# Moving VectorE's mixing weights and two engines' loop numbers behind the first block of a mixture-of-experts loop

## The chip, the cores and the metric

The kernel runs on one core of a Trainium2 chip. The metric is the device time of one execution in microseconds; where several runs are given, their median is meant.

## The reference

A decoder trunk of two layers over 512 tokens of width 1024, in float32. The first layer mixes tokens by a convolution, the second by dilated attention. Behind each mixer stands a mixture of experts: 16 experts in 4 groups, each token takes one group and the best two experts in it.

```python
def hierarchical_moe(h, r_grp, r_exp, w_gate, w_up, w_down):
    p_grp = jax.nn.softmax(t @ r_grp);  g_idx = argmax(p_grp);  p_top = p_grp[g_idx]
    sel = expert logits of the group g_idx
    top_v, top_i = lax.top_k(sel, 2)
    w_in = jax.nn.softmax(top_v, axis=-1) * p_top[:, None]     # the mixing weights
    a = t @ w_gate[e];  u = t @ w_up[e]
    y = sum over e of (silu(a) * u * gates[:, e]) @ w_down[e]
```

The mixing weights are two numbers a token, `w_in`. They are needed only when the experts' outputs are added up.

## The kernel before

The experts are computed in blocks of 128 token slots; each block has one expert. There are at least 16 blocks, and more where an expert has over 128 tokens; how many is known only when the routing has been computed on the chip. So the routing (`routing`, on VectorE) leaves three integers in SBUF, `two_i` and `last_i` (two columns), and each engine reads them into its own registers with `value_load`: `two`, `last` and `before`. `before` is the number of trips of the main loop, `last` the number of the last pair of blocks, `two` says whether the last pair is whole. SyncE, GpSimd and TensorE have their own loads; the change leaves these alone.

Every product is made in three passes: an operand is cut into a leading part (fp32r, made by ScalarE: `gate_lead`, `up_lead`, `rows_lead`, `down_lead`) and a trailing part (VectorE: `gate_trail`, `up_trail`, `rows_trail`, `down_trail`), and TensorE adds lead x lead, lead x trail and trail x lead. Blocks go in order 0, 1, 2, ...; block 0 has its gate and up products ahead of the loop (TensorE's `gate(0, 0)`, `up(0, 0)`). After that a `split_block(i, c)` takes, on each engine, the gate and up products of block 2i + c and the down product of the block before it. TensorE's order in it is: gate, transposed rows of the next block, first half of the down product, up, second half of the down product, transposition of the hidden values. Half a down product needs from ScalarE `hTh` and `wdh`, and from VectorE `hTl` (waited for at its start) and `wdl` (waited for ahead of its last four matmuls, L2081).

The engines run from instruction lists of their own and are tied only by semaphores. All instructions of an engine run in the order of its list, so a pause on VectorE delays all that stands behind it there. `wgh` is one buffer: ScalarE may refill it only when the gate product that reads it is done. VectorE's small steps in `mixing_weights` (L1561 to L1568) wait for each other through the semaphore of `steps`, so that its sequencer can't run ahead of them.

The loop's body (both `split_block(i, 1)` and `split_block(i, 2)`) is in a `Fori` loop of the engine. On VectorE and TensorE the loop began at pair 0; on ScalarE pair 0 was written out and the loop began at 1.

Of the kernel before, what the change touches and what calls it, by code (L numbers as in the profile page):

```python
# [47 lines left out]
E = 16  # L48
# [5 lines left out]
XB = 8  # L54
# [89 lines left out]
def build_program(nc, a):  # L144
# [7 lines left out]
    with ExitStack() as ctx:  # L152
# [3 lines left out]
        def sem(name):  # L156
            return ctx.enter_context(nc.semaphore(name))
# [148 lines left out]
        def rs(*dims, dt=F32):  # L306
            nonlocal o
            n = 1
            for d in dims:
                n *= d  # L310
            ap = cut(HTQf, o, *dims)
            o += n
            return ap.bitcast(dt) if dt != F32 else ap
# [47 lines left out]
        last_i = rs(2, dt=I32)  # L361
        two_i = rs(2, dt=I32)
# [100 lines left out]
        routed = Count(sem("routed"), L2, [1] * 2)  # L463
# [379 lines left out]
        def _(act):  # L843
# [145 lines left out]
            def moe_act(l):  # L989
# [13 lines left out]
                def gate_lead(b, n, used, qs=range(2)):  # L1003
                    if used is not None:
                        act.wait_ge(gate_mm[l], used)
                    lead(wg[b], wgh, wg_in[l][b], gh_done[l], n, qs)

                def up_lead(b, n, used):
                    if used is not None:
                        act.wait_ge(up_mm[l], used)  # L1010
                    lead(wu[b], wuh, wu_in[l][b], uh_done[l], n)

                def rows_lead(b, n, banks=0):

                    act.wait_ge(xgT_mm[l][b], n)
                    for q in range(2):
                        nc.scalar.activation(xgh[b][:, 4 * q:4 * q + 4, :], PS[ROW_BANKS[banks][q]][:, :].rearrange("p (a b) -> p a b", a=4),  # L1017
                                             ACT.Copy).then_inc(xh_done[l], 1)
# [1 line left out]
                gate_lead(0, 1, None)  # L1020
                up_lead(0, 1, None)
                rows_lead(0, 1)
                act.wait_ge(routed.sem, routed.at(l, 1))
                two = act.value_load(two_i[0:1, 0:1], min_val=0, max_val=1)
                last = act.value_load(last_i[0:1, 0:1], min_val=E // 2 - 1, max_val=(E + XB) // 2 - 1)
                before = act.value_load(last_i[0:1, 1:2], min_val=E // 2 - 2, max_val=(E + XB) // 2 - 2)

                def silu_gate(i, c):
                    act.wait_ge(gate_mm[l], 2 * i + (c + 1))
                    act.wait_ge(hid_done[l], 2 * i + (c + 1))  # L1030
                    nc.scalar.activation(sil, PS[0][:, :], ACT.Silu).then_inc(sil_done[l], 1)

                def down_lead(h, i, b):
                    nc.scalar.activation(wdh[:, :, :], wd[b][:, :, h * 512:(h + 1) * 512], ACT.Copy).then_inc(dh_done[l].sem, 1)  # L1034

                def split_block(i, c):
                    p, n = (c - 1) % 2, (c + 1) % 2
                    act.wait_ge(hT_mm[l], 2 * i + c)
                    nc.scalar.activation(hTh[:, :, :].rearrange("p a b -> p (a b)"), PS[2][:, :], ACT.Copy).then_inc(hTh_done[l].sem, 1)
                    act.wait_ge(wd_in[l][p], (i + 1) * 16)  # L1040
                    if isinstance(i, int) and i == 0 and c == 1:
                        act.wait_ge(y_cleared.sem, y_cleared.at(32 * (l + 1)))
                    down_lead(0, i, p)
                    silu_gate(i, c)
                    gate_lead(n, i + 2, None, [0])
                    act.wait_ge(down_half[l].sem, down_half[l].at(2 * i + c))
                    down_lead(1, i, p)
                    gate_lead(n, i + 2, None, [1])
                    if not isinstance(i, int):
                        act.wait_ge(y_stored[l][p], i * 16)  # L1050
                    nc.scalar.activation(yst[p][:, 0:512], PS[3][:, :], ACT.Copy)
                    rows_lead(n, i + 2)
                    up_lead(n, i + 2, 2 * i + (c + 1))
                    act.wait_ge(down_mm[l], 2 * i + c)
                    nc.scalar.activation(yst[p][:, 512:1024], PS[4][:, :], ACT.Copy).then_inc(y_done[l], 1)  # L1055
# [2 lines left out]
                gate_lead(1, 1, 1)  # L1058
                rows_lead(1, 1)
                up_lead(1, 1, 1)  # L1060
                for c in (1, 2):
                    split_block(0, c)
                with act.Fori(1, before) as i:
                    for c in (1, 2):
                        split_block(i, c)
# [128 lines left out]
        def _(dve):  # L1194
# [366 lines left out]
            def mixing_weights(l):  # L1561

                dve.wait_ge(gexp_done.sem, gexp_done.at(l, 2))
                steps.mark(V.tensor_reduce(gsum, gexp, AX, ALU.add))
                steps.step(V.tensor_scalar(gden, pick, 1.0, None, ALU.add))
                steps.step(V.tensor_tensor(gsum, gsum, gden, ALU.mult))
                steps.step(V.reciprocal(wt[0], gsum))
                steps.step(V.tensor_tensor(wt[1], wt[0], pick, ALU.mult))  # L1568

            def moe_dve(l):  # L1570
# [9 lines left out]
                def gate_trail(b, m, qs=range(2)):  # L1580
                    trail(wg[b], wgh, wgl[b], gh_done[l], gl_done[l], m, qs)

                def up_trail(b, m, qs=range(2)):
                    trail(wu[b], wuh, wul[b], uh_done[l], ul_done[l], m, qs)
# [8 lines left out]

                gate_trail(0, 0)
                rows_trail(0, 0)
                mixing_weights(l)
                before = dve.value_load(last_i[0:1, 1:2], min_val=E // 2 - 2, max_val=(E + XB) // 2 - 2)
                two = dve.value_load(two_i[0:1, 0:1], min_val=0, max_val=1)
                last = dve.value_load(last_i[0:1, 0:1], min_val=E // 2 - 1, max_val=(E + XB) // 2 - 1)
                up_trail(0, 0)  # L1600

                def place_last(b):
# [24 lines left out]
                def split_block(i, c, between=None):  # L1627
                    n, m = (c + 1) % 2, 2 * i + (c + 1)
                    dve.wait_ge(hTh_done[l].sem, hTh_done[l].at(2 * i + c))
                    V.tensor_tensor(hTl[:, :, :].rearrange("p a b -> p (a b)"), PS[2][:, :],  # L1630
                                    hTh[:, :, :].rearrange("p a b -> p (a b)").bitcast(F32), ALU.subtract).then_inc(hidT_done[l], 1)
                    down_trail(0, i, c)
                    gate_trail(n, m, [0])
                    down_trail(1, i, c)
                    gate_trail(n, m, [1])
                    hidden(i, c)
                    rows_trail(n, m)
                    up_trail(n, m, [0])
                    if between is not None:
                        between()  # L1640
                    up_trail(n, m, [1])
# [6 lines left out]
                hidden(0, 0)  # L1648
                rows_trail(1, 1)
                up_trail(1, 1)  # L1650
                with dve.Fori(0, before) as i:
                    for c in (1, 2):
                        split_block(i, c)
                split_block(before, 1, copy_hidT)
# [781 lines left out]
```

## Time and profile before

| what | value |
|---|---|
| median of 3 runs | 1479.34 us (1478.64 to 1480.61) |
| profiled execution, its own time | 1480.13 us |
| span of the profiled execution | 1478.3 us |
| TensorE busy | 1418.4 us, 96% |
| VectorE busy | 1129.0 us, 76% |
| ScalarE busy | 785.6 us, 53% |
| experts of the first layer, first gate product to the loop's end | from 239.88 us |
| experts of the second layer, the same | from 1158.47 us |

The span is the time between the first and the last instruction in the trace; the execution's own time is 1.83 us longer. Times of rows are in microseconds from the span's start. A name such as DVEq means the sequencer of VectorE (DVE), whose records are not counted as busy time. An instruction on VectorE or ScalarE may begin some 0.1 us before the one ahead of it has ended; so "start to start" is the measure of what an instruction takes in a row of them.

### The profile page before, as it was taken

The numbers are of one execution on the slowest core, as the hardware profiler recorded it, in microseconds if no ns is written. First come the engines' busy times: TensorE is split into PE (matmuls) and PEld (weight loads), VectorE is DVE, ScalarE is ACT, GpSimd is POOL, SyncE is SP. The second block draws the span as 40 slices with busy tenths as digits, with TensorE's granted clock in tenths as the row PEclk, the third lists the DMA queues.
The fourth block names the chain that finished last, engine by engine and source line by source line (L and its number), as shares of the span: only waits on it lengthen the run. The fifth ranks groups of instructions, "written<-read, shape, count | busy, mean of one in ns | idle before, by whom it ended". The sixth has DMA issues, their size and how long they took to land.

```text
span 1478.3 us, 20618 instructions
## 1 busy us (share of the span) xinstructions
PE 1418.4 (96%) x7272; PEld 1153.6 (78%) x7272; DVE 1129.0 (76%) x1648; ACT 785.6 (53%) x1024; POOL 459.6 (31%) x330
## 2 busy tenths in 40 slices
PE   7999997999999987999999999999998899999997
PEld 6889685888888855888888888888887588888863
DVE  6999828988888878765858667585753888888866
ACT  5211835777777736344252533424353677777733
POOL 0000015444444311432405233151402544444310
PEclk9999998999999999999999999999998999999999
DMA  5232517899999864222212122121546599999882
GB/s 217 88 136 90 225 43 280 347 373 380 381 379 394 352 239 154 86 71 71 85 57 99 57 85 71 57 99 57 200 144 241 199 363 381 382 385 376 319 314 109
DMA packets 52764, 309.85 MB, mean 210 GB/s; under 512 B 10544, under 2 KB 16432, under 8 KB 38896
## 3 DMA queue, kind: packets, MB, share of 16 engines
q1 hardware_dynamic: 42128, 291.48, 51.2%
q0 software_dynamic: 9792, 16.80, 3.1%
q10 hardware_dynamic: 800, 1.00, 0.2%
q8 instruction: 26, 0.43, 0.1%
q14 instruction: 18, 0.15, 0.0%
HBM read 299.27 MB, written 28.84 MB: 222 GB/s over the span
## 4 chain that ended last, share of the span: by engine, by line
PE 88%; DVE 6%; ACT 2%; issue 2%; DMA 1%; SPq 0%; DVEq 0%; ACTq 0%; POOLq 0%
PE PS L2188 5%; PE PS L2189 5%; PE PS L2190 5%; PE PS L2041 4%; PE PS L2042 4%; PE PS L2045 4%; PE PS L2030 4%; PE PS L2028 4%; PE PS L2029 4%; PE PS L2077 3%; PE PS L2078 3%; PE PS L2081 3%; PE PS L2204 3%; PE PS L2206 3%; PE PS L2205 3%; PE PS L2066 2%
## 5 line engine op out<-in xcount | busy, mean ns | idle before, releaser
L834 POOL TENSOR_TENSOR KQ<-rope_ab 64x512 f32<-64x512 f32 x96 | 173.7, 1809 | 320.0 <-DVE rope_ab L1703 316.4
L1578 DVE TENSOR_TENSOR wgl<-WR,wgh 128x2048 fp32r<-128x2048 f32 x66 | 150.9, 2293 | 38.8 <-ACT wgh L1001 38.8
L1112 ACT ACTIVATE wh<-wraw 128x1024 fp32r<-128x1024 f32 x76 | 80.2, 1057 | 176.0 <-PE PS L2190 171.7
L1578 DVE TENSOR_TENSOR wul<-WR,wuh 128x2048 fp32r<-128x2048 f32 x66 | 148.2, 2284 | 5.2 <-issue 5.2
L1625 DVE TENSOR_TENSOR wdl<-WR,wdh 128x2048 fp32r<-128x2048 f32 x56 | 128.1, 2287 | 24.3 <-ACT wdh L1034 24.3
L1703 DVE TENSOR_TENSOR rope_ab<-PS,rope_sb 32x512 f32<-32x512 f32 x192 | 131.9, 687 | 2.6
L1001 ACT ACTIVATE wuh<-WR 128x2048 fp32r<-128x2048 f32 x66 | 122.8, 1908 | 12.6 <-PE PS L2030 12.6
L1034 ACT ACTIVATE wdh<-WR 128x2048 fp32r<-128x2048 f32 x56 | 107.4, 1918 | 35.1 <-PE PS L2081 35.1
L1001 ACT ACTIVATE wgh<-WR 128x2048 fp32r<-128x2048 f32 x66 | 125.2, 1904 | 0.0
L1685 DVE TENSOR_TENSOR wl<-wraw,wh 128x1024 fp32r<-128x1024 f32 x76 | 94.6, 1245 | 31.6 <-ACT wh L1112 30.1
L2041 PE MATMUL PS<-wgh,xgh 128*128 128x512 f32 x264 | 107.5, 407 | 1.4 <-ACT xgh L1017 1.4
L2028 PE MATMUL PS<-wuh,xgh 128*128 128x512 f32 x264 | 103.0, 390 | 1.3 <-DVE wul L1578 1.3
L2042 PE MATMUL PS<-wgl,xgh 128*128 128x512 f32 x264 | 104.2, 395 | 0.0
L2029 PE MATMUL PS<-wul,xgh 128*128 128x512 f32 x264 | 102.7, 389 | 0.0
L2030 PE MATMUL PS<-wuh,xgl 128*128 128x512 f32 x264 | 102.7, 389 | 0.0
L771 POOL TENSOR_TENSOR idle<-ident_sb 128x1 f32<-128x1 f32 x30 | 20.9, 695 | 261.0 <-ACT SC L1055 248.7
L2077 PE MATMUL PS<-wdh,hTh 128*128 128x512 f32 x224 | 91.1, 407 | 0.0
L2078 PE MATMUL PS<-wdh,hTl 128*128 128x512 f32 x224 | 88.2, 394 | 0.0
L772 POOL DMA_INDIRECT y_dram<-SC,HTQ x30 | 79.4, 2646 | 5.3 <-issue 5.3
L2204 PE MATMUL PS<-HTh,wh 128*128 128x512 f32 x192 | 77.1, 402 | 0.0
L2206 PE MATMUL PS<-HTh,wl 128*128 128x512 f32 x192 | 74.9, 390 | 0.0
L2205 PE MATMUL PS<-HTl,wh 128*128 128x512 f32 x192 | 74.9, 390 | 0.0
(372 smaller groups left out, 3517.9 us busy)
## 6 DMA issues: line engine op xcount, KB each, us to landing
WR<-w_gate SPq DMA_DIRECT2D x33, 2048.0 KB, 11.5
WR<-w_up SPq DMA_DIRECT2D x33, 2048.0 KB, 8.9
WR<-w_down SPq DMA_DIRECT2D x33, 2048.0 KB, 11.5
wraw<-w_qkv SPq DMA_DIRECT2D x72, 512.0 KB, 3.3
WR<-w_in SPq DMA_DIRECT2D x8, 1024.0 KB, 4.9
xn_dram<-SC SPq DMA_DIRECT2D x8, 512.0 KB, 2.9
SC<-y_dram SPq DMA_DIRECT2D x8, 512.0 KB, 5.8
HT<-y_dram SPq DMA_DIRECT2D x8, 512.0 KB, 8.9
```

Source lines behind the costliest of these rows:

```text
L834: nc.gpsimd.tensor_tensor(to, cos, sin, ALU.add).then_inc(rope_done, 1)
L1001: nc.scalar.activation(dst[:, kts, :], src[:, kts, :], ACT.Copy).then_inc(done, 1)
L1578: V.tensor_tensor(lo[:, kts, :], raw[:, kts, :], hi[:, kts, :].bitcast(F32), ALU.subtract).then_inc(done, 1)
L1625: V.tensor_tensor(wdl[b][:, :, cols], wd[b][:, :, cols], wdh[:, :, :].bitcast(F32), ALU.subtract).then_inc(dl_done[l].sem, 1)
L1703: ins = V.tensor_tensor(rope_ab[d:d + 32, 2 * (t % 2) + 1, :], src[s:s + 32, :], rope_t[s:s + 32, tab + 1, :], ALU.mult)
L2028: M.matmul(dst, xgh[b][:, kt, :], hi[:, kt, :], start=kt == 0, stop=False)
L2029: M.matmul(dst, xgh[b][:, kt, :], lo[:, kt, :], start=False, stop=False)
L2030: ins = M.matmul(dst, xgl[b][:, kt, :], hi[:, kt, :], start=False, stop=kt == KT - 1)
L2041: M.matmul(PS[0][:, :], xgh[b][:, kt, :], wgh[:, kt, :], start=kt == 0, stop=False)
L2042: M.matmul(PS[0][:, :], xgh[b][:, kt, :], wgl[b][:, kt, :], start=False, stop=False)
L2077: M.matmul(to, hTh[:, ft, :], wdh[:, ft, :], start=ft == 0, stop=False)
L2078: M.matmul(to, hTl[:, ft, :], wdh[:, ft, :], start=False, stop=False)
```

## The change

VectorE: `mixing_weights` and the three `value_load` move from between `rows_trail(0, 0)` and `up_trail(0, 0)` to between `split_block(0, 1)` and `split_block(0, 2)`. For that the first pair is taken out of VectorE's loop and written out, and the loop begins at 1. ScalarE: its three `value_load`, with the wait for the routing, move from behind `rows_lead(0, 1)` to the same place, between its `split_block(0, 1)` and `split_block(0, 2)`. All of it is done in both layers.

```diff
--- before.py
+++ after.py
@@ -1020,10 +1020,6 @@
                 gate_lead(0, 1, None)
                 up_lead(0, 1, None)
                 rows_lead(0, 1)
-                act.wait_ge(routed.sem, routed.at(l, 1))
-                two = act.value_load(two_i[0:1, 0:1], min_val=0, max_val=1)
-                last = act.value_load(last_i[0:1, 0:1], min_val=E // 2 - 1, max_val=(E + XB) // 2 - 1)
-                before = act.value_load(last_i[0:1, 1:2], min_val=E // 2 - 2, max_val=(E + XB) // 2 - 2)
 
                 def silu_gate(i, c):
                     act.wait_ge(gate_mm[l], 2 * i + (c + 1))
@@ -1058,8 +1054,12 @@
                 gate_lead(1, 1, 1)
                 rows_lead(1, 1)
                 up_lead(1, 1, 1)
-                for c in (1, 2):
-                    split_block(0, c)
+                split_block(0, 1)
+                act.wait_ge(routed.sem, routed.at(l, 1))
+                two = act.value_load(two_i[0:1, 0:1], min_val=0, max_val=1)
+                last = act.value_load(last_i[0:1, 0:1], min_val=E // 2 - 1, max_val=(E + XB) // 2 - 1)
+                before = act.value_load(last_i[0:1, 1:2], min_val=E // 2 - 2, max_val=(E + XB) // 2 - 2)
+                split_block(0, 2)
                 with act.Fori(1, before) as i:
                     for c in (1, 2):
                         split_block(i, c)
@@ -1593,10 +1593,6 @@
 
                 gate_trail(0, 0)
                 rows_trail(0, 0)
-                mixing_weights(l)
-                before = dve.value_load(last_i[0:1, 1:2], min_val=E // 2 - 2, max_val=(E + XB) // 2 - 2)
-                two = dve.value_load(two_i[0:1, 0:1], min_val=0, max_val=1)
-                last = dve.value_load(last_i[0:1, 0:1], min_val=E // 2 - 1, max_val=(E + XB) // 2 - 1)
                 up_trail(0, 0)
 
                 def place_last(b):
@@ -1648,7 +1644,13 @@
                 hidden(0, 0)
                 rows_trail(1, 1)
                 up_trail(1, 1)
-                with dve.Fori(0, before) as i:
+                split_block(0, 1)
+                mixing_weights(l)
+                before = dve.value_load(last_i[0:1, 1:2], min_val=E // 2 - 2, max_val=(E + XB) // 2 - 2)
+                two = dve.value_load(two_i[0:1, 0:1], min_val=0, max_val=1)
+                last = dve.value_load(last_i[0:1, 0:1], min_val=E // 2 - 1, max_val=(E + XB) // 2 - 1)
+                split_block(0, 2)
+                with dve.Fori(1, before) as i:
                     for c in (1, 2):
                         split_block(i, c)
                 split_block(before, 1, copy_hidT)
```

## Rows read from the trace of the kernel before

**Rows 1.** The page: the chain that ended last, by engine.

```profile
PE 88%; DVE 6%; ACT 2%; issue 2%; DMA 1%; SPq 0%; DVEq 0%; ACTq 0%; POOLq 0%
```

**Rows 2.** Busy time by stretch, here one in the first layer's loop; then clock, DMA.

```profile
309.00:400.00 91.00, 91.00 (x431) 75.95 (x430) 80.84 (x52) 72.23 (x64) 42.58 (x31) 1.00 0.94 379
```

**Rows 3.** Timeline of VectorE, first layer, start of the experts (start, us, instruction, [idle before]).

```profile
241.46 0.16 DVE L1564 TENSOR_REDUCE HTQ<-HTQ 128x4 f32<-128x16 f32 x1
...
244.56 4.49 DVE L1578 TENSOR_TENSOR wul<-WR,wuh 128x2048 fp32r<-128x2048 f32 x2 [2.27 <-issue]
249.71 4.49 DVE L1578 TENSOR_TENSOR wgl<-WR,wgh 128x2048 fp32r<-128x2048 f32 x2 [0.66 <-ACT wgh L1001]
254.12 0.68 DVE L1619 TENSOR_TENSOR SC<-PS,SC 128x512 f32<-128x512 f32 x1
```

**Rows 4.** Timeline of VectorE, second layer, the same place.

```profile
1160.29 0.15 DVE L1564 TENSOR_REDUCE HTQ<-HTQ 128x4 f32<-128x16 f32 x1
...
1164.05 4.49 DVE L1578 TENSOR_TENSOR wul<-WR,wuh 128x2048 fp32r<-128x2048 f32 x2 [2.92 <-issue]
1168.46 4.49 DVE L1578 TENSOR_TENSOR wgl<-WR,wgh 128x2048 fp32r<-128x2048 f32 x2
1172.87 0.68 DVE L1619 TENSOR_TENSOR SC<-PS,SC 128x512 f32<-128x512 f32 x1
```

**Rows 5.** Timeline of TensorE in both layers, start of the experts.

```profile
254.86 0.75 PE L2057 MATMUL PS<-ident_sb,SC 128*128 128x128 f32 x4 [1.27 <-DVE SC L1619]
...
1164.05 1.04 PE L2018 MATMUL PS<-ident_sb,SC 128*128 128x128 f32 x8
1166.40 0.50 PE L2028 MATMUL PS<-wuh,xgh 128*128 128x512 f32 x1 [1.31 <-DVE wul L1578]
...
1173.61 0.75 PE L2057 MATMUL PS<-ident_sb,SC 128*128 128x128 f32 x4 [1.43 <-DVE SC L1619]
```

**Rows 6.** Timeline of ScalarE in both layers: the silu of the first block.

```profile
247.28 0.60 ACT L1031 ACTIVATE SC<-PS 128x512 f32<-128x512 f32 x1 [4.86 <-PE PS L2045]
...
1164.24 0.60 ACT L1031 ACTIVATE SC<-PS 128x512 f32<-128x512 f32 x1 [3.46 <-PE PS L2045]
```

**Rows 7.** Sequencer records by line: ns least/median/most, first and last start in us.

```profile
L1597 DVEq TENSOR_LOAD <-HTQ x2: 559/704/850, 242.3 to 1161.2; - x2
...
L1599 DVEq TENSOR_LOAD <-HTQ x2: 357/560/762, 243.9 to 1163.0; - x2
...
L626 SPq TENSOR_LOAD <-HTQ x58: 262/270/295, 241.8 to 1408.1; - x58
...
L1024 ACTq TENSOR_LOAD <-HTQ x2: 282/375/468, 239.2 to 1157.8; - x2
...
L1026 ACTq SEQ_ASSERT  x2: 18/18/18, 241.0 to 1159.4; - x2
```

**Rows 8.** Timeline of VectorE, first layer, between the first pair's two split blocks.

```profile
277.38 0.68 DVE L1630 TENSOR_TENSOR hTl<-PS,hTh 128x512 fp32r<-128x512 f32 x1
277.99 2.28 DVE L1625 TENSOR_TENSOR wdl<-WR,wdh 128x2048 fp32r<-128x2048 f32 x1
```

**Rows 9.** Timeline of TensorE, first layer, first half of the down product of split_block(0, 2).

```profile
279.59 0.48 PE L2077 MATMUL PS<-wdh,hTh 128*128 128x512 f32 x1
...
281.54 1.07 PE L2081 MATMUL PS<-wdl,hTh 128*128 128x512 f32 x4
```

**Rows 10.** Timelines of VectorE and of TensorE, second layer, the same place.

```profile
1196.69 2.28 DVE L1625 TENSOR_TENSOR wdl<-WR,wdh 128x2048 fp32r<-128x2048 f32 x1
...
1200.24 1.07 PE L2081 MATMUL PS<-wdl,hTh 128*128 128x512 f32 x4
```

**Rows 11.** Timeline of ScalarE, first layer: the silu of split_block(0, 2).

```profile
278.99 0.60 ACT L1031 ACTIVATE SC<-PS 128x512 f32<-128x512 f32 x1 [2.24 <-PE PS L2045]
```

**Rows 12.** Timeline of TensorE, first layer: first and ninth matmul of the first gate.

```profile
239.88 0.71 PE L2041 MATMUL PS<-wgh,xgh 128*128 128x512 f32 x1 [0.69 <-ACT xgh L1017]
...
243.38 0.42 PE L2041 MATMUL PS<-wgh,xgh 128*128 128x512 f32 x1
```


## The prediction

> **What bounds the kernel now.** I read the page first, and in it the chain that ended last: 88% of it is TensorE and 6% VectorE, nothing else is over 2% [rows 1]. Then the busy time by stretch: inside the experts' loop TensorE is busy for all of 91 us, with VectorE at 81 and ScalarE at 72 [rows 2]. So in the loop a pause of another engine costs nothing until it has used up the slack to the moment at which TensorE asks for its result, and beyond that it costs us for us, since TensorE has no idle time later in the loop in which to make it good. The change moves a pause on VectorE from ahead of the loop into it. The timelines of the two places therefore decide: where does TensorE stand for VectorE now, and how much slack is there at the new place.
>
> At the old place, VectorE pauses between `rows_trail(0, 0)` and `up_trail(0, 0)`: first layer from 241.46 to 244.56, **3.10 us** [rows 3], second layer from 1160.29 to 1164.05, **3.76 us** [rows 4]. The last 2.27 and 2.92 us of these, by the idle time in the same rows, are the three `value_load` with the sequencer's work around them; the rest, 0.83 and 0.84 us, is the five small steps of `mixing_weights`. The pause lies differently in the two layers. In the second, TensorE has its transposes at 1164.05 and then stands 1.31 us for `wul`, until 1166.40 [rows 5]; `gate_trail(1, 1)` follows on VectorE without a gap at 1168.46, and `hidden(0, 0)` (L1619) at 1172.87 [rows 4]; TensorE stands 1.43 us for it [rows 5]. In the first layer no such wait for `wul` appears, and VectorE is idle 0.66 us ahead of `gate_trail(1, 1)`, for ScalarE's `wgh` [rows 3]: there the pause is over before it can matter.
>
> **What taking the pause away is worth.** First layer: `gate_trail(1, 1)` begins at 249.71 because ScalarE may refill `wgh` only after the gate product; ScalarE's silu, which waits for the same product, begins at 247.28 [rows 6]. An earlier `up_trail` changes neither, so `hidden(0, 0)` stays at 254.12 and TensorE stands its 1.27 us as before [rows 5]. Worth 0. (The first layer's gate product is itself longer, for its clock, see below; it isn't touched.)
>
> Second layer: with `up_trail` started at 1160.29 its 4.49 us are over at 1164.8, before TensorE has finished its transposes (1164.05 + 1.04). Then the order of the first layer holds: ScalarE's silu, then `wgh`, then `gate_trail(1, 1)`, then `hidden(0, 0)`. In the first layer that took 254.12 - 247.28 = 6.84 us [rows 3, 6]; from the silu at 1164.24 [rows 6] it gives 1171.08 instead of 1172.87. **Gain 1.79 us**, the smaller of what TensorE would gain at `up` and what `hidden` allows. The loop that follows is TensorE's, and takes the gain along.
>
> **What the pause costs at its new place.** Ahead of it stands `up_trail(0, 2)`, behind it `split_block(0, 2)`: `hTl`, then the first `wdl`. VectorE has no gap there: neither `hTl` at 277.38 nor `wdl` at 277.99 has idle time ahead of it [rows 8]. `wdl` ends at 277.99 + 2.28 = 280.27, and TensorE asks for it at 281.54, for `hTl` at 279.59 [rows 9]. Slack 1.27 us for `wdl`; `hTl` ends at 277.38 + 0.68 = 278.06, slack 1.53. The second layer has the same: 1196.69 + 2.28 = 1198.97 against 1200.24, 1.27 [rows 10]. The steps of `mixing_weights` and the loads can't hide behind other work of VectorE, since each waits for the one ahead of it and the list goes on only after them. So the whole pause is added there, and with 0.04 us from an end on VectorE to the start on TensorE (254.12 + 0.68 against 254.86 is 0.06, so 0.04 to 0.06) the cost is pause + 0.04 - 1.27.
>
> First layer: 3.10 + 0.04 - 1.27 = **1.87 us**. TensorE would stand first about 1.6 us at L2077 for `hTl` (3.10 - 1.53 + 0.04), then 0.26 at L2081. Second layer: 3.76 + 0.04 - 1.27 = **2.53 us**. What is queued behind the pause on VectorE after `wdl` (the `wgl` halves, the second `wdl`, `hidden`) has its own idle time in each block, 81 us busy of 91 in the loop [rows 2], so it catches up within the block and TensorE is not made to wait again.
>
> Are the loads as long there? The DMA engines are much busier at the new place. The 58 loads that SyncE makes through the loops took 262 to 295 ns, so traffic alone doesn't lengthen them; VectorE's first load took 559 and 850, its third 357 and 762 [rows 7], and the idle time with them 2.27 and 2.92 [rows 3, 4]; I have no row that says why. Bounds: at SyncE's 270 ns the first layer's first load loses 0.29 and its third 0.09, which makes 3.10 a pause of 2.7; at 850 ns for all, the second layer's third load gains 0.09 and its second at most 850 - 262, 0.59, which makes 3.76 one of 4.4. Costs for a layer 1.5 and 3.2. I take each layer's own pause, as the nearest row. The Trainium skill (DMA: Bandwidth & Descriptors, Latency and other measured facts) gives a `tensor_load` a floor of about 600 ns; SyncE's 58 loads speak against it. By that floor, three loads at 0.6 us would make the pause some 3.7 us in both layers, and the sum below 3.15 instead of 2.61.
>
> **The rest costs nothing.** ScalarE: its loads ran from 239.2 to 241.0 in the first layer and 1157.8 to 1159.4 in the second, 1.6 to 1.8 us [rows 7], ahead of 4.86 and 3.46 us in which it waited for the gate product [rows 6]: taking them away gains nothing. At the new place they delay `hTh` and `wdh` by as much; ScalarE waits 2.24 us between `wdh` and the silu of the block [rows 11], so `wdh` ended at 276.75 and would end at 278.6, still before 279.59. With that cover gone each us would count, but `hTh` isn't what is late: VectorE comes to `hTl` later anyway. The wait for `routed` that moves with the loads has long been met. Writing out a pair on VectorE saves one set of loop instructions and costs code; neither is on a path. No DMA is moved; GpSimd and SyncE have their own loads.
>
> **Sum.** 1.87 + 2.53 - 1.79 = **+2.61 us**. On the profiled execution's own 1480.13 (span 1478.3 + 1.83) that is 1482.7; its median of the runs, 1479.34, lies 0.8 lower and becomes 1481.95, which I forecast. Below 0.2%, or 2.96 us, I count two versions as not told apart; 2.61 lies inside, but close to the edge. Bounds of the sum: 2 x 1.5 - 1.79 = +1.2 and 2 x 3.2 - 1.79 = +4.6.
>
> **Rivals.**
> *The pause is swallowed.* If at the new place the pause fell under the slack of 1.27 us, only the gain would be left: 1479.34 - 1.79 = 1477.55. For it: ScalarE's loads do run ahead of its engine's work. Against it: VectorE's loads stand behind steps that wait for their own ends, and even the shortest loads leave 2.7 us. It is the case on the other side; it decides from a pause below about 2.1 us in each layer (2 x (2.1 - 1.23) = 1.8). Chance 8%, and 3% more for a gain beyond 0.2% by something the rows don't show.
> *The stall costs TensorE its clock.* The first layer's gate product took 3.50 us for its first eight matmuls [rows 12], against 1.95 for eight at full speed [rows 9]: 1.6 us lost at the lower of two granted levels, after the gaps of the routing. If a stall of 1.9 or 2.5 us did this once a layer, the sum would be 2.61 + 3.2 = +5.8, 1485.1. Against it: after the gaps of 1.27 and 1.43 us [rows 5] the loop ran at full clock, and the new stall comes in the middle of dense work. The Trainium skill (TensorE: Matmul & The Clock Gate, Part 1) has the clock follow how busy the array has been recently, which leaves both open. Chance 7%.
> *No gain at the old place.* Something else holds `hidden(0, 0)` in the second layer, for instance `wgh` later than in the first: +4.4, 1483.7. The order of work is the same in both layers, which speaks against it. Chance 5%.
> *Forecast:* pauses much as now, 77%, of which about a third (25%) lies beyond +2.96 by the loads' length.
>
> **Numbers.** Slower by over 0.2%: 25% + 7% + 4% of the third rival = 36%. Faster by over 0.2%: 3% and 1% of the swallowed case = 4%. Within: the rest, 60%. The range takes in the loads' bounds and the swallowed case's upper part: 1479.0 to 1484.4.
>
> **What would show it.** In the trace after: no wait of TensorE for `wul` in the second layer, `hidden(0, 0)` some 1.8 us sooner behind the gate's start; in each layer a wait of TensorE for `hTl` at L2077 of 1.6 to 2.3 us and a short one at L2081; VectorE's small steps at about 277.4 in the first layer. The forecast is wrong if the loads at the new place are much shorter or longer than 3.1 to 3.8 us with the steps, if the granted clock falls behind the stall, or if the loop after it doesn't hold TensorE busy throughout.

## The result and the profile after

The changed kernel takes 1484.69 us, the median of 8 runs (1483.43 to 1488.12); the kernel before takes 1479.64 us in the 8 runs beside it (1478.64 to 1480.66). The ratio is 1.0035, with a 95% interval of 1.0026 to 1.0044: slower by 5.2 us, 3.8 to 6.5. The forecast was +2.6 us and a range that ended at 1484.4. The sign is right, the time lies just outside the range, and the loss is twice the sum. The runs also lie further apart than those beside them, 4.7 us instead of 2.0; but the kernel before, run more often beside the experiments, lay 4.3 to 5.6 us apart, so this alone says little.

The profiled execution took 1485.55 us, with a span of 1483.7, 5.4 more than before. Behind the old place the lines of VectorE are 4 lower: L1619 of before (`hidden`) is L1615, L1630 (`hTl`) is L1626, L1625 (`wdl`) is L1621; on TensorE all lines are 2 higher. The chain that ended last has moved from TensorE to VectorE, to DMA and, for the first time, to GpSimd (POOL) [rows 1]:

```profile
PE 85%; DVE 7%; ACT 2%; DMA 2%; issue 2%; POOL 1%; DVEq 0%; SPq 0%; POOLq 0%; ACTq 0%
```

Timeline of TensorE after, the places where it stands at the experts' start and at the down product, first layer and then second:

```profile
238.78 0.50 PE L2043 MATMUL PS<-wgh,xgh 128*128 128x512 f32 x1 [0.69 <-ACT xgh L1017]
...
252.14 0.75 PE L2059 MATMUL PS<-ident_sb,SC 128*128 128x128 f32 x4 [1.27 <-DVE SC L1615]
...
261.08 1.16 PE L2020 MATMUL PS<-ident_sb,SC 128*128 128x128 f32 x8 [2.72 <-DMA SC<-xn_dram,HTQ]
...
282.04 0.47 PE L2079 MATMUL PS<-wdh,hTh 128*128 128x512 f32 x1 [1.97 <-issue]
...
1161.22 0.80 PE L2043 MATMUL PS<-wgh,xgh 128*128 128x512 f32 x1 [0.69 <-ACT xgh L1017]
...
1176.15 0.75 PE L2059 MATMUL PS<-ident_sb,SC 128*128 128x128 f32 x4 [1.27 <-DVE SC L1615]
...
1203.42 0.47 PE L2079 MATMUL PS<-wdh,hTh 128*128 128x512 f32 x1 [2.32 <-issue]
```

Four things are to be seen. The wait for `wul` in the second layer is gone [rows 5]. The down product of `split_block(0, 2)` now waits 1.97 us in the first layer and 2.32 in the second, where before there was no wait [rows 9]; the rows name no releaser, but both times `hTl` ends on VectorE 0.11 us before the wait is over (281.24 + 0.69 and 1202.62 + 0.69, rows below). In the first layer the transposes of block 2's gathered rows (L2020) wait 2.72 us for the gather, a wait that the prediction did not look at. And the first gate product of the second layer starts at the lower granted clock (its first matmul takes 0.80 us), while that of the first layer (0.50) does not; before it was the other way round [rows 12]. That product isn't touched by the change and its clock differs from execution to execution: in the 14 profiles of this record it began at the lower level, or fell to it, in 9 first layers and in 5 second ones.

To put the 5.4 us together, two more rows of TensorE's timeline before are needed, the transposes of block 2's rows in the first layer and the start of the down product in the second:

```profile
260.91 1.10 PE L2018 MATMUL PS<-ident_sb,SC 128*128 128x128 f32 x8
...
1198.29 0.48 PE L2077 MATMUL PS<-wdh,hTh 128*128 128x512 f32 x1
```

Difference after minus before at each mark: first gate -1.10 (238.78 against 239.88); block 2's transposes +0.17; down product +2.45 (282.04 against 279.59); second layer's first gate +2.75; transposes of block 0's hidden values +2.54; down product +5.13; end +5.4. So from mark to mark: 1.27 us lost up to the gathered rows (TensorE was 2.72 earlier at block 0's hidden values than before, 1.10 of it from ahead of the gate product and 1.62 by the clock, and lost all of it and more in the wait), **2.28 at the first layer's down product**, 0.30 behind it, -0.21 in the second layer's start, **2.59 at its down product** and 0.27 behind it. The -0.21 is the gain of 1.79 and a loss of about 1.57 by the clock: gate start to silu took 7.34 us instead of 5.77. From silu to `hidden` it is 6.85 us, the forecast 6.84. ScalarE's silu, then VectorE's `hidden`:

```profile
1168.56 0.60 ACT L1027 ACTIVATE SC<-PS 128x512 f32<-128x512 f32 x1 [5.61 <-PE PS L2047]
...
1175.41 0.68 DVE L1615 TENSOR_TENSOR SC<-PS,SC 128x512 f32<-128x512 f32 x1
```

VectorE's timeline after at the new place, first steps of the mixing weights and what follows them, first and second layer:

```profile
277.61 0.16 DVE L1564 TENSOR_REDUCE HTQ<-HTQ 128x4 f32<-128x16 f32 x1
...
278.34 0.17 DVE L1568 TENSOR_TENSOR HTQ<-HTQ 128x4 f32<-128x4 f32 x1
281.24 0.69 DVE L1626 TENSOR_TENSOR hTl<-PS,hTh 128x512 fp32r<-128x512 f32 x1 [2.74 <-issue]
281.85 2.28 DVE L1621 TENSOR_TENSOR wdl<-WR,wdh 128x2048 fp32r<-128x2048 f32 x1
...
1198.64 0.16 DVE L1564 TENSOR_REDUCE HTQ<-HTQ 128x4 f32<-128x16 f32 x1
...
1202.62 0.69 DVE L1626 TENSOR_TENSOR hTl<-PS,hTh 128x512 fp32r<-128x512 f32 x1 [3.07 <-issue]
```

The pause is 281.24 - 277.61 = 3.63 us and 1202.62 - 1198.64 = 3.98 us, against 3.10 and 3.76 at the old place [rows 3, 4]. The three loads behind the steps are longer than they were (the same view as [rows 7]):

```profile
L1649 DVEq TENSOR_LOAD <-HTQ x2: 317/434/551, 278.5 to 1199.6; - x2
...
L1650 DVEq TENSOR_LOAD <-HTQ x2: 354/533/712, 279.5 to 1200.6; - x2
...
L1651 DVEq TENSOR_LOAD <-HTQ x2: 672/731/790, 280.1 to 1201.6; - x2
```

GpSimd at the experts' start in the first layer, before. Its list there is: clear y rows (copy, a dummy operation, descriptors) twice, then the same three steps for the gather of block 2's rows (L761):

```profile
241.58 0.20 POOL L784 COPY HTQ<-HTQ 128x1 uint32 x1
241.86 0.19 POOL L787 TENSOR_TENSOR idle<-ident_sb 128x1 f32<-128x1 f32 x1
242.59 1.01 POOL L788 DMA_INDIRECT y_dram<-SC,HTQ  x1 [0.54 <-issue]
...
244.70 3.09 POOL L761 DMA_INDIRECT SC<-xn_dram,HTQ  x1 [0.55 <-issue]
```

And after:

```profile
240.49 2.20 POOL L784 COPY HTQ<-HTQ 128x1 uint32 x1
242.78 2.13 POOL L787 TENSOR_TENSOR idle<-ident_sb 128x1 f32<-128x1 f32 x1
245.06 1.02 POOL L788 DMA_INDIRECT y_dram<-SC,HTQ  x1 [0.15 <-issue]
...
247.17 3.04 POOL L761 DMA_INDIRECT SC<-xn_dram,HTQ  x1 [0.56 <-issue]
```

Before, VectorE was paused from 241.46 to 244.56, and the copy, the dummy operation and the descriptors of the second clear took 0.20, 0.19 and 1.01 us. After, VectorE runs its two `wul` halves there; the copy ends with the first of them (240.49 + 2.20) and the dummy operation with the second. The gather is issued 8.39 us behind the gate's start instead of 4.82.

### The profile page after: what moved, and what is told of

The parts are those of the page before. It is cut to its first block, busy times and chain, and to the rows that moved or that the text cites. A ratio compares the mean times of both kernels' runs of the same rounds, so it can differ in the third digit from the quotient of the medians.

```text
span 1483.7 us, 20594 instructions
## 1 busy us (share of the span) xinstructions
PE 1416.1 (95%) x7272; PEld 1151.0 (78%) x7272; DVE 1129.8 (76%) x1648; ACT 785.8 (53%) x1024; POOL 459.7 (31%) x330
## 4 chain that ended last, share of the span: by engine, by line
PE 85%; DVE 7%; ACT 2%; DMA 2%; issue 2%; POOL 1%; DVEq 0%; SPq 0%; POOLq 0%; ACTq 0%
PE PS L2190 5%; PE PS L2191 5%; PE PS L2192 5%; PE PS L2043 4%; PE PS L2044 4%; PE PS L2047 4%; PE PS L2030 3%; PE PS L2032 3%; PE PS L2031 3%; PE PS L2083 3%; PE PS L2079 3%; PE PS L2080 3%; PE PS L2206 3%; PE PS L2208 3%; PE PS L2207 3%; PE PS L2068 2%
## 5 line engine op out<-in xcount | busy, mean ns | idle before, releaser
L1621 DVE TENSOR_TENSOR wdl<-WR,wdh 128x2048 fp32r<-128x2048 f32 x56 | 128.2, 2289 | 27.6 <-ACT wdh L1030 27.6
## 6 DMA issues: line engine op xcount, KB each, us to landing
WR<-w_down SPq DMA_DIRECT2D x33, 2048.0 KB, 12.2
```

The source lines that it names most:

```text
L1621: V.tensor_tensor(wdl[b][:, :, cols], wd[b][:, :, cols], wdh[:, :, :].bitcast(F32), ALU.subtract).then_inc(dl_done[l].sem, 1)
```

## The experiments

Each was run in 5 rounds beside the kernel before; differences are the ratio's interval times 1479. **Stall** is the theory that the new pause, less 1.23 us of slack (1.27 less the 0.04 of the prediction), is all that is lost. **GpSimd** is the theory that VectorE's old pause was also of use, since GpSimd's small operations got through in it.

**The change in one layer alone.** In the first: the work is moved only `if l == 0`.

> The change in the first layer alone. Two theories. Stall: all that the change costs is VectorE's pause between the two split blocks; it was 3.63 us in the profile after, less 1.23 of slack, so +2.4 to +2.6 us against the kernel before, with runs as close together as those of before (2 us). Gather: VectorE's old pause also let GpSimd's small copies through ahead of the gather of block 2's rows; without it the gather lands later than TensorE asks for it in this layer (a wait of up to 2.7 us on L2020 in the profile after), so more than the stall: +3.3 to +5, with runs some 3 us or more apart, and the wait on the gathered rows in the trace.

Measured +3.8 us (2.2 to 5.3), runs 3.8 us apart, and a wait of 2.27 us for the gathered rows in the trace. Stall alone is too small at its middle, though not outside the interval. The runs of the kernel before beside it lay 5.2 us apart, so the scatter tells nothing; and the wait for the gather comes in this layer for another reason too (see What stays open).

> The change in the second layer alone. Here the gather is not late in the profile after, so both theories say the same: the pause of 3.98 us less 1.23 of slack costs 2.6 to 2.9 us, the gain at the old place is 1.8 us: +0.8 to +1.1 us. Nearer to +2.7 would mean that the gain isn't there.

Measured +2.8 us (0.9 to 4.6), runs 7.5 us apart. The gain is there: no wait for `wul`, and the transposes of block 0's hidden values stand 14.96 us behind the gate's start though that gate ran at the lower clock, which costs some 1.6 (before, 15.14 at the full clock). The time is nonetheless nearer to the +2.7 of a loss without the gain, though its interval reaches down to the forecast; the runs of the kernel before beside it lay 5.2 us apart. That something else is lost in this layer in some executions is a guess so far.

**ScalarE's part alone.**

> ScalarE's part of the change alone; VectorE as in the kernel before. Both theories: within 0.3 us of the kernel before, since ScalarE's loads have cover at the old place and at the new one. If ScalarE's part has a share in the loss, it shows here.

Measured +0.3 us (-0.9 to 1.6). No share of ScalarE in the loss is to be seen, and one above 1.6 us lies outside the interval.

**Most of the work behind the loop.** At the new place VectorE only reads `before`:

```diff
                 split_block(0, 1)
-                mixing_weights(l)
                 before = dve.value_load(...)
-                two = dve.value_load(...)
-                last = dve.value_load(...)
                 split_block(0, 2)
...
                 rows_trail(1, 2 * before + 3, 1)
+                mixing_weights(l)
+                two = dve.value_load(...)
+                last = dve.value_load(...)
```

> The kernel after, but on VectorE only the one number that the loop needs (before) is read between the first two split blocks; the mixing weights and the other two numbers come behind the loop, where VectorE waits some 10 us for TensorE anyway. Stall theory: the pause at the new place is about 0.7 to 1 us, under its slack of 1.23, so nothing is lost and the gain of the second layer stays: -1.8 us against the kernel before. Gather theory: the second layer's 1.8 us are gained, but in the first layer TensorE still waits for the gathered rows as in the kernel after: -1.8 + 1 to 3, so between -1 and +1.5 us, with runs 2 to 4 us apart.

Measured +0.7 us (-0.7 to 2.4), runs from 1477.22 to 1485.58. In its trace VectorE has no gap at the new place and TensorE no wait at the down product, and the second layer's gain is whole. TensorE's timeline, first gate and transposes of block 0's hidden values:

```profile
1158.73 0.50 PE L2043 MATMUL PS<-wgh,xgh 128*128 128x512 f32 x1 [0.69 <-ACT xgh L1017]
...
1172.09 0.75 PE L2059 MATMUL PS<-ident_sb,SC 128*128 128x128 f32 x4 [1.27 <-DVE SC L1615]
```

13.36 us, against 15.14 before (1173.61 [rows 5] less 1158.47): 1.78 gained in this execution, and yet no time won in the middle of the runs: the -1.8 of the stall theory lies outside the interval. The stall theory can't say where it went.

**GpSimd's order.** On the version above, the gather goes ahead of the two clears:

```diff
-                for b in range(2):
-                    clear(b)
-                for b in range(2):
-                    pool.wait_ge(gathered[l][b], 16)
-                    gather(b, 1)
+                pool.wait_ge(gathered[l][0], 16)
+                gather(0, 1)
+                for b in range(2):
+                    clear(b)
+                pool.wait_ge(gathered[l][1], 16)
+                gather(1, 1)
```

> The version with the weights and two numbers behind the loop (no stall between the split blocks), and GpSimd issues the gather of block 2's rows ahead of its two clears of y rows instead of behind them. Stall theory alone: the order on GpSimd is off the path, so the same as without it, within 0.5 us. Gather theory: the late gather is what takes back the second layer's gain and spreads the runs over 8 us; with it first the version comes to -1.8 us against the kernel before or a little better, and its runs lie within some 3 us. Third theory, clears: if it is the clears (which ScalarE waits for) that come late without VectorE's old pause, this order makes it worse: above +1 us, spread kept.

Measured +3.0 us (1.0 to 4.9), runs 10.8 us apart. The gather theory as I had put it falls, and the third one holds: now the clears come too late. In the trace TensorE stands for `wdh` at the first down product, 2.19 us in the first layer and 1.09 in the second, and goes on in the first at the lower clock. The same order on the kernel before:

> The kernel before with only the gather put ahead of the clears. Gather theory: in the profile before the gathered rows land just as TensorE asks for them, so there is little to win: 0 to -0.7 us. Stall theory: 0.

Measured +1.2 us (-0.1 to 2.4), where the gather theory had 0 to -0.7. Its trace shows what the clears hold up: ScalarE's `wdh`, which lies where the zeros are read from, and behind it TensorE (first layer):

```profile
260.49 1.91 ACT L1035 ACTIVATE wdh<-WR 128x2048 fp32r<-128x2048 f32 x1 [4.78 <-DMA y_dram<-SC,HTQ]
...
262.45 0.50 PE L2078 MATMUL PS<-wdh,hTh 128*128 128x512 f32 x1 [2.40 <-ACT wdh L1035]
```

So both the clears and the gather are near the path, and what matters is how fast GpSimd gets through the whole list. With it late, either may be what TensorE waits for.

**An empty pause in the first layer.** On the version with the work behind the loop, `dve.wait_ge(scol_done[l], 1)` is put ahead of `up_trail(0, 0)` for `l == 0`.

> The same version in the old order of GpSimd, but in the first layer VectorE waits, ahead of its first up_trail, until GpSimd has done its small copy ahead of the gather: the old pause without the old work, some 3 us long. Gather theory: in the first layer GpSimd is as early as in the kernel before, so -1.3 to -1.8 us, and the runs closer together than the 8 us of the version without the hold. Stall theory: no difference from the version without the hold, +0.5 us. If the second layer's GpSimd is what comes late, the spread stays.

Measured 0.0 us (-1.6 to 1.5), runs 4.6 us apart instead of 8.4; the forecast of the GpSimd theory, -1.3 to -1.8, is at the edge. The median doesn't tell it from the version without the pause. But its trace holds what the others had not shown, in the second layer, where VectorE has no pause. GpSimd's descriptors for the first clear, VectorE's two `wul` halves, and TensorE at block 2's rows:

```profile
1158.46 5.30 POOL L788 DMA_INDIRECT y_dram<-SC,HTQ  x1 [0.88 <-issue]
...
1158.38 4.48 DVE L1578 TENSOR_TENSOR wul<-WR,wuh 128x2048 fp32r<-128x2048 f32 x2
...
1179.36 1.16 PE L2022 MATMUL PS<-ident_sb,SC 128*128 128x128 f32 x8 [3.19 <-DMA SC<-xn_dram,HTQ]
```

The descriptors, which took 1.01 us beside a paused VectorE, last until 0.90 us after both large subtractions, 5.30 us. The gather is issued 12.92 us behind the gate, and TensorE waits 3.19 us. What started it lies further ahead: the small copy before these descriptors, begun 1.29 us after the start of `gate_trail`'s two subtractions, took 3.24 us here, to the end of the second; in the kernel before, begun at the same distance, it took 1.03, to the end of the first. With the old pause behind it such a delay is made good (not seen in a trace); without it the next step runs into `up_trail`.

**Loads ahead of the steps.** On the kernel after, only the order at the new place is turned round:

```diff
                 split_block(0, 1)
-                mixing_weights(l)
                 before = dve.value_load(...)
                 two = dve.value_load(...)
                 last = dve.value_load(...)
+                mixing_weights(l)
                 split_block(0, 2)
```

> The kernel after with the order at the new place turned round on VectorE: the three loads first, the mixing weights behind them. The version with one load alone at this place showed no gap on VectorE at all. Theory: a load runs in the sequencer while the engine still works on what is queued, and costs only because in the kernel after it stands behind steps that wait for their own ends. Then the pause shrinks from 3.6 and 4.0 us to the steps' 0.85, which is under the slack: no wait at the down product, and the time is that of the version with the work behind the loop, -0.5 to +1 us against the kernel before. Rival: three loads take the engine's time wherever they stand; then the pause stays 3.6 to 4.0 us and the time is that of the kernel after, +4 to +5 us.

Measured -0.4 us (-1.9 to 1.0), where the kernel after has +5.2: the pause at the new place is what that kernel loses by. VectorE at the new place:

```profile
279.76 0.17 DVE L1564 TENSOR_REDUCE HTQ<-HTQ 128x4 f32<-128x16 f32 x1
...
280.49 0.16 DVE L1568 TENSOR_TENSOR HTQ<-HTQ 128x4 f32<-128x4 f32 x1
280.69 0.69 DVE L1626 TENSOR_TENSOR hTl<-PS,hTh 128x512 fp32r<-128x512 f32 x1
```

The pause is 280.69 - 279.76 = 0.93 us, under the slack, and TensorE doesn't wait at the down product. The loads ran at 276.4 to 278.3, beside `wul`. Here they cost no time; in the kernel after, where they stand behind steps that wait for their own ends, they do.

The same trace, first layer, shows a cost that the theories had left out. TensorE at block 2's rows:

```profile
260.48 1.97 PE L2020 MATMUL PS<-ident_sb,SC 128*128 128x128 f32 x8 [2.82 <-DMA SC<-xn_dram,HTQ]
```

After this wait of 2.82 us the eight transposes take 1.97 us instead of 1.04: TensorE is at the lower of its two clock levels (granted clock 0.50 from 260 to 266), and from them to the up product it needs 6.52 us, where the profile after needed 3.78. So a late gather can cost 2.7 us of clock on top of its wait. The clock also fell in the version below with VectorE kept busy (both layers, 1.4 and 1.3 us) and in the one above with the gather first and the work behind the loop; it did not after 2.72 us in the profile after, nor after the 3.19 above.

**The pause twice.** On the kernel after, the old work stays at the old place as well.

> The kernel after, with the mixing weights and the three loads of VectorE also kept at the old place: the old pause stays and the new one is added. Nothing changes for GpSimd or for the start of the experts; what is left is the price of the new pause by itself. Both theories: +4.9 to +5.5 us against the kernel before (2.6 for the first layer and 2.9 for the second, less 0.3), and runs as close together as those of before. If it is nearer to +3.5, the stall is cheaper than read from the trace and GpSimd's share in the loss is larger.

Measured +3.8 us (2.4 to 5.5), runs 2.2 us apart. Below the forecast, and for a reason in its trace: the second time the loads are shorter. TensorE's transposes and its wait at the down product, then VectorE's pause, all in the second layer:

```profile
1174.72 0.75 PE L2063 MATMUL PS<-ident_sb,SC 128*128 128x128 f32 x4 [1.47 <-DVE SC L1619]
...
1201.03 0.47 PE L2083 MATMUL PS<-wdh,hTh 128*128 128x512 f32 x1 [1.39 <-issue]
...
1197.20 0.16 DVE L1564 TENSOR_REDUCE HTQ<-HTQ 128x4 f32<-128x16 f32 x1
...
1200.24 0.69 DVE L1630 TENSOR_TENSOR hTl<-PS,hTh 128x512 fp32r<-128x512 f32 x1 [2.15 <-issue]
```

The pause is 3.04 us here (3.03 in the first layer). Two times 3.04 - 1.23 are 3.6, with 0.3 behind the waits (as in the profile after) 3.9: the price of the stall is what the trace says, pause less slack. And with the old pause kept the scatter is small.

**Loads first at the old place.** On the kernel before, the same turn at the old place.

> The kernel before with only the order at the old place turned round on VectorE: loads first, mixing weights behind. The pause shrinks from 3.1 and 3.8 us to some 0.9. Stall theory: the second layer gains 1.8 us, -1.8 against the kernel before. GpSimd theory: the gain is taken back in part, since GpSimd finds VectorE busy: -0.5 to +1 us, runs more than 4 us apart.

Measured +0.3 us (-1.3 to 2.1), runs from 1475.96 to 1483.99. Here there is no new place at all, only a shorter pause: the steps' 0.9 us, and ahead of them 1.00 and 0.46 us in which VectorE still stands for the loads, 1.9 and 1.4 together instead of 3.1 and 3.8: the fastest run is 1.2 us under the fastest of before's (1477.13), the slowest 1.8 over the slowest, and nothing is won in the middle. Its trace has the whole gain (block 0's hidden values 13.37 us behind the gate's start in the second layer), the second clear as early as before, 2.95 us, and the gather late, 8.02 us.

**Busy instead of paused.** On the version with the loads first, VectorE does 3.4 us of extra subtractions at the old place (their results are never read):

```diff
+                for q, n in ((0, 4), (1, 2)):
+                    dve.wait_ge(uh_done[l], q + 1)
+                    steps.mark(V.tensor_tensor(cut(SC, 5632 - 1024 * q, n, F), wu[0][:, 4 * q:4 * q + n, :],
+                                               wuh[:, 4 * q:4 * q + n, :].bitcast(F32), ALU.subtract))
+                steps.wait()
                 up_trail(0, 0)
```

> The version with the loads ahead of the mixing weights at the new place (no stall left at the down product). At the old place VectorE does two extra large subtractions (2048 and 1024 columns, some 3.4 us, into rows nobody reads) ahead of up_trail, instead of the pause of the kernel before. For TensorE VectorE is then as late as before, so the second layer's gain is gone; but VectorE is never still, and GpSimd's small copies and the writing of its descriptors have to wait for it. GpSimd theory: +1.5 to +3 us against the kernel before, runs 5 us or more apart, second clear 6 us or more behind the gate's start instead of 2.7 to 2.9. Stall theory alone: the same as the kernel before, within 0.5 us, runs as close as before's.

Measured +4.3 us (2.8 to 5.6), runs 6.9 us apart. GpSimd's descriptors for the two clears and the gather in the second layer, then TensorE at block 2's rows, second layer and first:

```profile
1161.77 4.24 POOL L788 DMA_INDIRECT y_dram<-SC,HTQ  x1 [0.88 <-issue]
...
1169.84 3.06 POOL L788 DMA_INDIRECT y_dram<-SC,HTQ  x1 [0.15 <-issue]
...
1175.14 1.06 POOL L761 DMA_INDIRECT SC<-xn_dram,HTQ  x1 [0.55 <-issue]
...
1184.62 1.97 PE L2024 MATMUL PS<-ident_sb,SC 128*128 128x128 f32 x8 [3.50 <-DMA SC<-xn_dram,HTQ]
...
262.63 1.97 PE L2024 MATMUL PS<-ident_sb,SC 128*128 128x128 f32 x8 [2.79 <-DMA SC<-xn_dram,HTQ]
```

**Paused, and empty.** On the same version, `dve.wait_ge(scol_done[l], 1)` ahead of `up_trail(0, 0)` in both layers.

> The same version, but at the old place VectorE does nothing until GpSimd has made its small copy ahead of the gather, in both layers: the old pause with none of the old work in it. GpSimd theory: the same as the kernel before, -0.5 to +0.5 us, and the runs within 3.5 us of each other instead of the 6 us of the version without the wait; second clear at 2.7 to 2.9 us behind the gate's start. Rival (the spread comes from something else about the moved work): the runs stay 6 us apart.

Measured +0.6 us (-0.7 to 1.8), runs 5.0 us apart, all but one within 2.8. GpSimd's descriptors of the second clear, and VectorE's `wul` behind the empty pause, second layer:

```profile
1161.30 1.02 POOL L788 DMA_INDIRECT y_dram<-SC,HTQ  x1 [0.54 <-issue]
...
1162.55 4.49 DVE L1578 TENSOR_TENSOR wul<-WR,wuh 128x2048 fp32r<-128x2048 f32 x2 [2.30 <-POOL HTQ L755]
```

The comparison that carries the argument is the busy version against the kernel before. VectorE is about as late for TensorE in both (block 0's hidden values stand 15.01 us behind the gate's start in the second layer, against 15.14; `up_trail` starts 5.03 and 5.28 us behind it, against 4.68 and 5.58), and no stall is left at the down product. Stall alone allows 0.5 us; measured were 4.3, with the gather issued 12 and 15 us behind the gate and TensorE waiting for it in both layers: in the profile, 6.5 us longer than that of before, these two waits alone are 6.29. That a GpSimd made late by a busy VectorE costs time is thereby shown.

Busy against paused, 4.3 against 0.6, intervals apart, points the same way but holds more than that: the empty pause was shorter, `up_trail` started 4.20 us behind the gate in the second layer and the hidden values stood at 13.76, so that some 1.3 us of the difference there is VectorE's own. The pause was also over before the gather's own steps: they ran beside `up_trail`, and the gather was issued at 6.5 and 6.7 us, not at 4.8 and 5.0. The runs were 5.0 us apart and not within the forecast 3.5; the kernel before beside them lay 4.3 apart.

## Why the prediction was wrong

**The stall: mechanism right, size too small.** The place, the slack (1.27 us for `wdl`) and the waits for `hTl` came as forecast: 1.97 and 2.32 us at L2077's counterpart, forecast 1.6 to 2.3. Of the short second wait for `wdl` the trace shows no row. The term that was mis-sized is "I take each layer's own pause": 3.63 and 3.98 us instead of 3.10 and 3.76, inside the bounds of 2.7 to 4.4. In the profile the two down products with what follows cost 2.58 and 2.86, together 5.4, against 4.40 in the sum; 0.75 of the difference is the longer pauses. Why VectorE's loads took 0.3 us in some places and up to 0.85, and 1.1 once, stays open; they were shorter, mostly 0.30, where the same numbers had been loaded shortly before or where they ran beside a large operation.

**"The loads can't hide": half right.** They can't behind the steps. I gave the reason and did not see the remedy in it: in front of the steps they cost nothing.

**The gain: right for one clock level, and in part luck.** 1.79 us forecast; 1.78 in the version with the work behind the loop, and 6.85 us from silu to `hidden` against 6.84. But it rests on the second layer's gate product having been at the full clock in the profile before. Where that product is at the lower level, silu comes some 1.6 us later and hides the old pause. With the gather first on the kernel before, whose old pause was 2.78 us there:

```profile
1159.66 0.79 PE L2042 MATMUL PS<-wgh,xgh 128*128 128x512 f32 x1 [0.69 <-ACT xgh L1018]
...
1174.59 0.75 PE L2058 MATMUL PS<-ident_sb,SC 128*128 128x128 f32 x4 [1.27 <-DVE SC L1620]
```

That is 14.93 us with the pause; the kernel after, at the lower level too, has 1176.15 - 1161.22 = 14.93 without it. In the same way the first layer's gain of 0 holds for the lower level, at which it was profiled: at the full level that layer stood at 14.18 us with the pause (the same trace) and at 13.36 without it (the profile after), 0.8 us apart. So the gain is up to 1.8 us in one layer and up to 0.8 in the other, by execution.

**The first layer's old place, "Worth 0": wrong, and so was "GpSimd and SyncE have their own loads".** This is the step that failed. I asked who on TensorE waits for VectorE's pause to end, and never who runs while it lasts. Taking the pause away made GpSimd 3.5 us later in both layers, and 8 in one layer of the version with the pause in the first layer only, and behind GpSimd stand the clears (for ScalarE) and the gather (for TensorE). What it costs, worked out as measured less stall and gain: kernel after 5.2 - 5.4 + 1.8 = 1.6 us; work behind the loop 0.7 + 1.8 = 2.5; loads first 1.4; loads first at the old place 2.1. Each is uncertain by about 1.5, and takes the gain at 1.8, which not every execution has. The kernel after's 1.6 and the 1.0 by which the stall was too small make up the 2.6 us that the sum lacked; the 1.6 is a remainder, so that they add up is no proof. That a GpSimd held up by VectorE costs time is shown by the busy version, where its gather is issued 7 and 10 us later than before; how much of the 1.6 is GpSimd's is not.

**The rivals.** The pause was not swallowed. The stall at the down product did not cost the clock: the first matmul behind it took 0.47 us, and the granted clock there was 1.00. But that rival's mechanism was there, at a wait that the prediction did not have, that for the gather or the clears: four of the nine waits of 2.1 to 3.5 us in these traces were followed by the lower clock. There was a gain at the old place.

**What stays open.** The single late gather of a profile doesn't follow its issue in the first layer: it landed between 21.0 and 22.4 us behind the gate with the issue at 4.8 and at 8.4 alike (16.8 in one), while in the second layer it landed at 13.2 for an issue at 5.0, 16.8 for 8.6 and 22.8 to 24.8 for 12.9 and 15.3 (in the first layer of the busy version 23.8 for 12.2). In the first layer two loads of `w_down` are queued shortly before it, which may be why; that wasn't tried.

So the first layer's wait of 2.72 us in the profile after is not shown to come from the 3.5 us by which the gather was issued later. It goes rather with the gate's clock: with the gate at full clock TensorE reaches block 2's rows 19.6 to 19.8 us behind its start, and waited 2.72, 2.27, 2.82 and 2.14 us, the last with the pause kept and the gather issued at 6.5; at the lower clock it gets there at 21.0 to 21.8 and waited 0 to 1.0 us, as in the profile before, for every issue up to 8.4. A profile of the kernel before, in GpSimd's old order, with the first gate at full clock is not on record. No profile tells, either, in how many executions the clock falls behind such a wait. In the second layer an issue 3.5 us later cost no wait in any profile; the waits came with the gather issued 12.9 and 15.3 us behind the gate.

No version was found that is faster than the kernel before by more than can be measured: loads first at the new place comes nearest, at -0.4 us.

## What to carry to other kernels

Before a pause of an engine is closed, look at what every other engine does during it; an idle stretch of VectorE may be one that GpSimd needs. Put a register load ahead of steps that wait for their own ends, not behind them: beside queued work it cost nothing here. Read a gain or a wait only together with the granted clock of the product ahead of it: one profile shows one of two cases. And when a kernel's runs begin to scatter after a change while one profile looks clean, compare with as many runs of the old kernel, then suspect a wait that is only sometimes met late, and provoke it (here, by keeping the neighbour busy on purpose).

## What the hardware showed that was not expected

A GpSimd copy of 128x1 took 0.20 us beside a paused VectorE and 2.20 us beside a VectorE subtraction of 128x2048, ending with it. Writing the descriptors of an indirect DMA took 1.01 us beside none, some 3 us beside one and 5.30 us beside two such subtractions. By the Trainium skill (SBUF — State Buffer, Who interferes with whom) a VectorE instruction with two inputs in SBUF contends with a GpSimd instruction that reads SBUF; the copies agree. The same section infers that `tensor_tensor` doesn't hold up the generation of descriptors; for these indirect DMAs the 3 and 5.30 us say that it does.

The load of one integer into a VectorE register took from 0.30 to 1.1 us, and from 0.31 to 1.1 within one kernel; on SyncE the 58 loads in the loops took 0.26 to 0.30 [rows 7], but one at an experts' start in the profile before 0.48. The granted clock of the first gate product was at its lower level in the first layer of one execution and in the second of another, with 1.6 us for it each time. Of nine waits of TensorE for the gather or the clears, four (2.19, 2.79, 2.82 and 3.50 us) were followed by work at the lower level (granted clock 0.50 to 0.60 there) and five (2.14, 2.27, 2.40, 2.72 and 3.19 us) were not: the length of the wait alone doesn't say which.
